# Second FFN of a hybrid decoder block: operand sums on GpSimd with two block sets, another order of the down passes, residual rows by quadrants, and PSUM copies of weights from the third pair on

## What is computed

```
gate, up = split(h @ w_up)            # w_up 1024 x 5632
y = (silu(gate) * up) @ w_down        # w_down 2816 x 1024
```

## Time and profile before

| | us |
|---|---|
| median of 3 runs (lowest, highest) | 2317.22 (2316.52, 2319.8) |
| the profiled execution | 2315.68 |
| its span in the profile | 2313.8 |
| TensorE busy (share of the span) | 2233.2 (97%) |
| VectorE busy | 1639.1 (71%) |
| ScalarE busy | 954.7 (41%) |
| GpSimd busy | 604.8 (26%) |
| mean granted TensorE clock | 0.987 |

### The profile page before, as it was taken

How to read it: one execution, slowest core, us unless ns; L and a number is a source line. 1 busy time by engine, 2 the same in 40 slices (tenths; PEclk the granted TensorE clock), 3 DMA queues, 4 the chain that set the end, 5 groups by cost and what they waited for, 6 DMA issues and landing times.

```text
span 2313.8 us, 32138 instructions
## 1 busy us (share of the span) xinstructions
PE 2233.2 (97%) x10370; PEld 1839.2 (79%) x10370; DVE 1639.1 (71%) x2145; ACT 954.7 (41%) x1555; POOL 604.8 (26%) x680
## 2 busy tenths in 40 slices
PE   7999999999999999999999899999999999999998
PEld 6788888888788887777787677887877888887886
DVE  5877777655555899999898737653496777765667
ACT  5555555445543122222223122334445555553444
POOL 2888999400000000000000150000333455541000
PEclk9999999999999999999999899999999999999999
DMA  6224444386763234444335432545445566658664
GB/s 167 73 82 133 143 141 139 121 274 194 256 198 123 89 121 151 127 126 136 105 112 180 153 125 78 164 152 185 164 141 180 201 204 204 204 204 299 195 193 173
DMA packets 298523, 370.61 MB, mean 160 GB/s; under 512 B 26457, under 2 KB 198577, under 8 KB 298064
## 3 DMA queue, kind: packets, MB, share of 16 engines
q1 hardware_dynamic: 279376, 300.24, 40.6%
q0 software_dynamic: 19056, 69.42, 8.4%
q10 hardware_dynamic: 16, 0.00, 0.0%
HBM read 259.73 MB, written 107.50 MB: 159 GB/s over the span
## 4 chain that ended last, share of the span: by engine, by line
PE 72%; DVE 19%; issue 4%; DMA 3%; ACT 2%; SPq 1%; POOL 0%; DVEq 0%; ACTq 0%; POOLq 0%
PE PU L1283 10%; PE PU L1285 10%; PE PU L1284 10%; DVE XT L2282 8%; PE PU L1224 5%; PE PU L1226 5%; PE PU L1225 5%; PE PU L1164 3%; PE PU L1163 3%; PE PU L1165 3%; PE PD L1163 3%; PE PD L1164 3%; PE PD L1165 3%; DVE TMP L2360 1%; PE PD L1358 1%
## 5 line engine op out<-in xcount | busy, mean ns | idle before, releaser
L1224 PE MATMUL PU<-Hhi,Whi 128*128 128x512 f32 x896 | 355.6, 397 | 9.8 <-DVE Hlo L2308 6.2
L1226 PE MATMUL PU<-Hhi,Wlo 128*128 128x512 f32 x896 | 351.7, 393 | 0.0
L1225 PE MATMUL PU<-Hlo,Whi 128*128 128x512 f32 x896 | 351.5, 392 | 0.0
L2282 DVE SCALAR_TENSOR_TENSOR XT<-XT,wq 128x1024 f32<-128x1024 f32 x240 | 309.3, 1289 | 7.8
L1043 POOL TENSOR_TENSOR RT<-XT 128x512 f32<-128x512 f32 x2 | 2.9, 1448 | 869.6 <-DMA XT<-d_conv 869.5
L1224 PEld LDWEIGHTS PU<-Hhi,Whi 128*128 128x128 f32 x896 | 170.1, 190 | 49.1 <-DVE Hlo L2308 7.8
L1225 PEld LDWEIGHTS PU<-Hlo,Whi 128*128 128x128 f32 x896 | 170.3, 190 | 35.4 <-issue 0.7
L1226 PEld LDWEIGHTS PU<-Hhi,Wlo 128*128 128x128 f32 x896 | 169.8, 189 | 36.0
L1283 PE MATMUL PU<-Hhi,Dhi 128*128 128x512 f32 x480 | 188.2, 392 | 5.6 <-ACT s1b L1630 5.6
L1285 PE MATMUL PU<-Hhi,Dlo 128*128 128x512 f32 x480 | 187.9, 391 | 0.0
L1284 PE MATMUL PU<-Hlo,Dhi 128*128 128x512 f32 x480 | 187.9, 391 | 0.0
(11 more groups left out here) (401 smaller groups left out, 5268.5 us busy)
## 6 DMA issues: line engine op xcount, KB each, us to landing
d_act<-G SPq DMA_DIRECT2D x88, 256.0 KB, 2.1
XT<-in_w_ffn_down SPq DMA_DIRECT2D x88, 256.0 KB, 3.3
XT<-d_act SPq DMA_DIRECT2D x88, 256.0 KB, 3.5
Wraw<-in_w_ffn_up SPq DMA_DIRECT2D x80, 256.0 KB, 4.5
XT<-in_w_ffn_up SPq DMA_DIRECT2D x80, 256.0 KB, 4.3
Wraw<-in_w_in SPq DMA_DIRECT2D x32, 512.0 KB, 6.0
Wraw<-d_sb SPq DMA_DIRECT2D x55, 256.0 KB, 2.7
TAB<-in_w_ffn_down POOLq DMA_DIRECT2D x11, 1024.0 KB, 5.3
```

Source lines behind the costliest of these rows:

```text
L1224: mm(o_, Whi[s][:, side, k, :], Hhi[:, k, hs[h]], start=k == 0, stop=False)
L1225: mm(o_, Whi[s][:, side, k, :], Hlo[:, k, hs[h]], start=False, stop=False)
L1226: last = mm(o_, Wlo[s][:, side, k, :], Hhi[:, k, hs[h]], start=False, stop=k == KT - 1)
L2282: stt(CVb, z_, w_, CVb, ALU.mult, ALU.add).then_inc(m["conv"], 1)
```

## The change

- PSUM copies: pairs 0 and 1 (those that are unrolled, with integer numbers) now both use SBUF for the low part; the copies to PSUM begin with the third pair. Both FFNs.
- `plain_act(r0, g0, 1, 1)` is issued one subtraction (`minus(2, 2, 1)`) earlier on VectorE. Both FFNs.
- The sums on GpSimd start when the weights of pair 1 are split, and use two block sets, XT[:, 6:8] and TAB in turn; the load for take k+2 is issued behind the sums of take k.
- D_ORD begins 3, 5, 7 instead of 7, 5, 3; pass 0 waits for weight sums step by step and for saved activations, pass 1 for activation sums.
- The residual rows come in four quadrants of 1 MB, behind steps (0,4), (0,7), (1,4) and (2,4); `gather` waits for them in passes 1, 2 and 4. One group of final squares moves from pass 3 to pass 2.

The core of the diff:

```diff
-D_ORD = (7, 5, 3, 4, 1, 2, 6)
+D_ORD = (3, 5, 7, 4, 1, 2, 6)
+D_ROWS = ((0, 1), (1, 1), (0, 0), (1, 0))
...
+            if p == 0:
+                sp.wait_ge(sb_st, 48 * (t + 1))
             sp.wait_ge(rd_lo, n - (RING - 1))
             sp.dma_start(raw_d(FFN2, slot), weights).then_inc(rd_raw[slot], 16)
             if p == 0:
+                sp.wait_ge(act_saved[0], 16 * (FT + 2 * t + 1))
+            if p == 1:
                 sp.wait_ge(sa_st, 48 * (t + 1))
             sp.wait_ge(ra_lo, n - (FFN2.z0 - FFN2.a0 + RING - 1))
...
-        sp.wait_ge(sb_st, 48 * FI)
...
+        ROWS_AT = ((0, 4), (0, 7), (1, 4), (2, 4))
+
+        def rows_after_mix(h, dh):
             sp.wait_ge(x_st, 16 * 2 * J)
             sp.wait_ge(u_prod, 7 * 2 * NSP)
-            load_rows(FFN2, h, d_x2)
+            sp.wait_ge(sa_st, 48 * (FI - 1))
+            sp.dma_start(XT[:, 4 * h:4 * h + 4, hs[dh]], d_x2[4 * h:4 * h + 4, :, hs[dh]].rearrange("j c d -> c j d"))\
+                .then_inc(xr_ld, 16)
...
-                if (p, t) in ((0, 6), (1, 6)):
-                    rows_after_mix(p)
+                if (p, t) in ROWS_AT:
+                    rows_after_mix(*D_ROWS[ROWS_AT.index((p, t))])
...
+        set_of = lambda k: (XT[:, 6:8, :].rearrange("p j n -> p (j n)"), TAB[:, 0:4 * HW])[k % 2]
+        TAKES = [("w", 0)] + [t for c in range(FI) for t in ((("w", c + 1),) if c + 1 < FI else ()) + (("a", c),)]
+        made = lambda k, kind: 48 * sum(1 for t in TAKES[:k] if t[0] == kind)
+
+        def stored(k):
+
+            wait(pool, sb_st, made(k, "w"))
+            wait(pool, sa_st, made(k, "a"))
+
+        def load_take(k):
+
+            kind, c = TAKES[k]
+            stored(max(k - 1, 0))
+            if kind == "w":
+                src = w_ffn2_down[0][2 * c * P:(2 * c + 2) * P].rearrange("(a p) n -> p a n", p=P)
+            else:
+                for h in range(2):
+                    pool.wait_ge(act_saved[h], 16 * (FT + 2 * c + 2))
+                src = rows_p(d_act[2 * c:2 * c + 2])
+            pool.dma_start(set_of(k).rearrange("p (a n) -> p a n", a=2), src).then_inc(pool_ld[k % 2], 16)
...
+        def take(k):
+
+            kind, c = TAKES[k]
+            blocks = set_of(k)
+            b0, b1, b2, b3 = [at4(blocks, i) for i in range(4)]
+            halves = lambda a: blocks[:, a * HW:(a + 2) * HW].rearrange("p (a n) -> p a n", a=2)
+            pool.wait_ge(pool_ld[k % 2], 16 * (k // 2 + 1 + (0 if k % 2 else KT)))
+            stored(k)
...
+            if k + 2 < len(TAKES):
+                load_take(k + 2)
 
         pool.wait_ge(rd_lo, FFN2.z0)
-        weight_sums(0)
-        for c in range(FI):
-            if c + 1 < FI:
-                weight_sums(c + 1)
-            act_sums(c)
+        pool.wait_ge(u_lo, 7 * (UBASE[FFN2] + 2))
+        pool.wait_ge(t_lo, 8)
+        for k in range(2):
+            load_take(k)
+        for k in range(len(TAKES)):
+            take(k)
...
-                    if (p, t) == (3, 7):
-                        fin_squares(0, 1, 2, 0)
+                    if (p, t) == (2, 7):
+                        fin_squares(0, 1, 1, 0)
...
-            if not (isinstance(p, int) and p == 0):
-                if isinstance(p, int) and p == 1 and POS[x] <= 3:
-                    act.wait_ge(c_in, 8)
-                    act.wait_ge(*norm_at("nf1" if S is FFN1 else "nf2", "lo", 2 * KT))
-                else:
-                    act.wait_ge(u_lo, q * 7 + HELD_BEFORE[POS[x]])
+            if not isinstance(p, int):
+                act.wait_ge(u_lo, q * 7 + HELD_BEFORE[POS[x]])
...
-                        if t == 2 and p in (1, 3):
-                            dve.wait_ge(xr_ld, {1: 80, 3: 96}[p])
+                        if t == 2 and p in (1, 2, 4):
+                            dve.wait_ge(xr_ld, {1: 96, 2: 112, 4: 128}[p])
...
-            if not (isinstance(p, int) and p == 0):
-                dve.wait_ge(u_hc, q * 7 + (POS[x] - (7 if S is FFN1 else 14)))
+            if not isinstance(p, int):
+                dve.wait_ge(u_hc, q * 7 + (POS[x] - (14 if S is FFN1 else 28)))
...
             minus(3, 2, 3)
+            plain_act(r0, g0, 1, 1)
             dve.wait_ge(t_add, t0 + 6)
             minus(2, 2, 1)
-            plain_act(r0, g0, 1, 1)
```

More of the change, by code:

```diff
@@ L338, in build @@
     ba_saved, ca_saved, rot_saved = sem("ba_saved"), sem("ca_saved"), sem("rot_saved")
-    small_saved, pool_ld = sem("small_saved"), sem("pool_ld")
+    small_saved, pool_ld = sem("small_saved"), sems("pool_ld", 2)
     norm = {k: sem("norm_" + k) for k in ("sq", "rs", "xn", "tr", "hi", "lo")}
@@ L736, in _ @@
             store_half(FFN2, NSP - 1, h)
-        def rows_after_mix(h):
+        ROWS_AT = ((0, 4), (0, 7), (1, 4), (2, 4))
+        def rows_after_mix(h, dh):
             sp.wait_ge(x_st, 16 * 2 * J)
             sp.wait_ge(u_prod, 7 * 2 * NSP)
-            load_rows(FFN2, h, d_x2)
+            sp.wait_ge(sa_st, 48 * (FI - 1))
+            sp.dma_start(XT[:, 4 * h:4 * h + 4, hs[dh]], d_x2[4 * h:4 * h + 4, :, hs[dh]].rearrange("j c d -> c j d"))\
+                .then_inc(xr_ld, 16)
         def store_out(h):
@@ L979, in tile_table @@
             r4 = slice(q * PR, (q + 1) * PR)
-            pool.dma_start(small4, d_small[:, :, r4, :]).then_inc(pool_ld, 16)
+            pool.dma_start(small4, d_small[:, :, r4, :]).then_inc(pool_ld[0], 16)
             pw_ = [[PW[:, a, 0:nt, r4].rearrange("p t r -> p r t").unsqueeze(3).to_broadcast([P, PR, nt, SG])
@@ L1014, in tile_table @@
             step(g.tensor_copy(M8q, M8[:, r4]))
-            pool.wait_ge(pool_ld, q * 16 + 16)
+            pool.wait_ge(pool_ld[0], q * 16 + 16)
             cs = TAB[:, T_COS:T_M8].rearrange("p (a r c) -> p a r c", a=2, c=C)
@@ L1052, in _ @@
         pool.dma_start(GF, norm_final_g.partition_broadcast(P)).then_inc(b_["fin_ld"], 16)
-        blocks = TAB[:, 0:4 * HW].rearrange("p (a n) -> p a n", a=2)
-        b0, b1, b2, b3, extra1, extra2 = [at4(TAB, i) for i in range(6)]
+        extra1, extra2 = at4(TAB, 4), at4(TAB, 5)
         extras = TAB[:, 4 * HW:6 * HW].rearrange("p (a n) -> p a n", a=2)
-        halves = lambda a: TAB[:, a * HW:(a + 2) * HW].rearrange("p (a n) -> p a n", a=2)
         rows_p = lambda ap: ap.rearrange("a p n -> p a n")
[L1060 to L1065, removed]
@@ L1067, in weight_sums @@
-        def weight_sums(c):
-            take(w_ffn2_down[0][2 * c * P:(2 * c + 2) * P].rearrange("(a p) n -> p a n", p=P), (c, max(c - 1, 0)), max(2 * c, c + 1))
-            step(g.tensor_tensor(extra1, b0, b3, ALU.add))
[L1071 to L1091, removed]
@@ new lines, in take @@
+        def take(k):
[5 more added lines that the diff above has]
+            stored(k)
+            step(g.tensor_tensor(extra1, b0, b3, ALU.add))
+            if kind == "w":
+                step(g.tensor_tensor(extra2, b2, b3, ALU.add))
+                pool.dma_start(rows_p(d_sb[c, B_T1:B_T7 + 1]), extras).then_inc(sb_st, 16)
+                step(g.tensor_tensor(b2, b2, b0, ALU.subtract))
+                step(g.tensor_tensor(b3, b1, b3, ALU.subtract))
+                pool.dma_start(rows_p(d_sb[c, B_T4:B_T3 + 1]), halves(2)).then_inc(sb_st, 16)
+                step(g.tensor_tensor(b1, b0, b1, ALU.add))
+                pool.dma_start(d_sb[c, B_T6], b1).then_inc(sb_st, 16)
+            else:
+                step(g.tensor_tensor(extra2, b0, b2, ALU.add))
+                pool.dma_start(rows_p(d_sa[c, A_S1:A_S5 + 1]), extras).then_inc(sa_st, 16)
+                step(g.tensor_tensor(b0, b1, b0, ALU.subtract))
+                step(g.tensor_tensor(b1, b1, b3, ALU.add))
+                pool.dma_start(rows_p(d_sa[c, A_S6:A_S2 + 1]), halves(0)).then_inc(sa_st, 16)
+                step(g.tensor_tensor(b2, b2, b3, ALU.subtract))
+                pool.dma_start(d_sa[c, A_S7], b2).then_inc(sa_st, 16)
+            if k + 2 < len(TAKES):
+                load_take(k + 2)
```

## The result

| | before | after |
|---|---|---|
| median, us (lowest, highest; 11 runs each) | 2317.22 (2315.3, 2320.54) | 2323.97 (2318.64, 2328.19) |
| ratio after / before, 95% interval | | 1.0024 [1.0015, 1.0033] |
| profiled execution, us | 2315.68 | 2324.92 |
| its span, us | 2313.8 | 2322.9 |
| mean granted TensorE clock | 0.987 | 0.985 |

The changed kernel is slower by 0.24% by the ratio (the medians differ by 6.75 us, 0.29%): inside the range (2309.0 to 2326.5), 5.4 us above the predicted 2318.6, and just over the 0.2% line.

A forecast was written before the change was run, and what follows sets the result against it. TensorE was busy 97% of the span, so only its idle or slow time could be won. Terms -1.3 - 5.7 + 8.4 = +1.4 us gave a median of 2318.6 us, 8 in 10 range 2309 to 2326.5.

The forecast's parts named there:

- (e): End of GpSimd's queue: last activation load stands ahead of block 9's sums, which start 2091.7 and land 2104.4 us.
- (f): Pass 0: SP's row wait holds step 5's operands; TensorE idles 13.2 us plus 2.2 slow matmuls, 8.4 us lost.
- (a): plain_act move, both FFNs: 1.32 us stop goes, VectorE's chain 0.6 us later, first FFN's pair 1 0.3 us later.
- (b): First FFN, pair 1 without PSUM copies: product 7 starts at 109.7, not 111.02, 1.3 us gained; 0.5 lost if clock falls.
- (c): Second FFN start without GpSimd's sums: product 7 of pair 1 starts at 1731.7, not 1737.44; 5.7 us gained.
- (d): Two block sets: a GpSimd take costs 14 us until caught up, some 20 before; TensorE indifferent, nothing taken.
- slower by VectorE: Rival: in the catch-up, 1731 to about 1890, denser sums make TensorE wait each pair; +8 us, 2326.6; chance 0.13.
- more than 2 us between 1760 and 2080: Sign that the forecast is wrong: TensorE idling more than this in the second FFN's up products.
- (g): Other moves, final squares a pass earlier and rows in four pieces: no effect, TensorE runs through from 2115.
- The faster one: Rival: smaller row loads remove the old stop in pass 0, nothing replaces it; 2303.2, milder case 2310.2; chance 0.17.
- The rival with a second stop: Rival: rows and late stores ahead of step 8 stop TensorE again, clock falls; +5 us, 2323.8; chance 0.12.
- the edits do nothing: Rival: the start is bound by pair 1's DMA, (b) and (c) fall; +8.4 us, 2325.6; chance 0.05.

The follow-up runs named there:

- Both experiments on it: The two runs last load behind (2314.37 us) and rows late (2315.74 us), each one edit to the changed kernel.
- before with copies from the third pair: Kernel before, only the copies to PSUM beginning at the third pair, GpSimd's sums in their old place: 2318.26 us, ratio 1.0007.
- plain_act back: Changed kernel with the plain block's multiplication put back behind the subtraction: 2322.74 us, ratio 1.0011.
- joined: Changed kernel with the last activation load behind block 9's sums, first two row loads behind (0,9) and (1,0), plain_act in its old place: 2306.46 us, 0.9947.
- joined gated: The joined kernel, GpSimd's sums of takes 11 to 19 also held until VectorE has made S16 of the coming pair: 2304.34 us, 0.9944.
- last load behind: Changed kernel, only GpSimd's load of activation block 10 moved behind the sums of block 9: 2314.37 us, ratio 0.9982.
- rows late: Changed kernel, only the first two row loads and their wait moved behind steps (0,9) and (1,0): 2315.74 us, ratio 0.9986.
- sums gated: The last load behind kernel, GpSimd's sums of takes 11 to 19 held until S16 of the coming pair is made: 2311.91 us, 0.9976.
- before with plain_act early: Kernel before, only plain_act(r0, g0, 1, 1) issued one subtraction earlier: 2324.45 us, ratio 1.0028.
- copies back: Changed kernel with the PSUM copies of pair 1 restored: 2325.07 us, ratio 1.0028.

## Why the prediction was near, and where it failed

The forecast (+1.4 us) was the sum -1.3 - 5.7 + 8.4. Against its own execution after had +9.1, the medians of all runs differ by 6.75, and the interval of the ratio allows 3.5 to 7.6.

- **(e), (f), the turn: right.** Block 9's sums from 2091.7 (measured 2091.88), landed 2104.4 (SP goes on at 2103.65), TensorE on at 2113 (2113.04), idle 13.2 (13.34), slow matmuls 2.2 (2.6). +8.4 against +9.3 in the ledger. Both experiments on it confirm the cause.
- **(a), (b) and (c) in one table.** Time from the first matmul of pair 0 to ScalarE's copy of pair 2's first product, less that of before, in us. A star marks a kernel whose granted clock fell behind the wait at product 7 of pair 1.

| kernels | first FFN | second FFN |
|---|---|---|
| pair 1 from SBUF, plain_act late: before with copies from the third pair | -1.4 | +4.3* |
| the same, sums late: plain_act back, joined, joined gated | -1.1, -1.3, -1.5 | -4.1*, -5.8, -5.6 |
| pair 1 from SBUF, plain_act early, sums late: after, last load behind, rows late, sums gated | +0.8*, +1.4*, -0.7, +1.2* | -3.3*, -5.3, -5.2, -3.6* |
| pair 1 through PSUM, plain_act early: before with plain_act early; copies back (sums late) | +1.4; +2.5 | +5.0*; -4.1 |

- **(c), the start of the second FFN: mechanism right, and the size nearly so where the clock held.** Product 7 of pair 1 was put at 1731.7 and began at 1732.36, 5.1 us earlier than before where 5.7 was written. Last load behind and rows late, the same code up to there, then lead by 5.3 and 5.2 us at pair 2. After leads by 3.3, since behind the 2.26 us wait the clock fell. The text had bounded this for (b) and forgot it for (c).
- **(b): mechanism right, the bound came true.** Where plain_act stays late, the first FFN is 1.1 to 1.5 us shorter in four kernels. The 1.3 of the text counts (a)'s delay in; with that delay and a held clock 0.7 is left (rows late). In after product 7 began at 110.59 instead of 109.7, of which 0.5 us stands before pair 0 begins (72.49, in before 72.01); then the clock fell behind the wait of 2.08, which is the bound that the text gives. The seven splits of pair 1 took 0.69 to 0.81 us in the first FFN of after, 0.3 us too much in all, so the 2.6 us that the weighing names did not come. In the second FFN the part alone loses 4.4 us, in the state that the kernel before leaves.
- **(a): undersized.** The delay of VectorE's chain is there as described (T3lo 0.5 us later from pair 0's start), but it costs 0.6 us in the first FFN where the clock held (rows late against the four with plain_act late), not 0.3. In the other three with plain_act early the clock fell too, which makes it 2 to 3 us. The medians of after and plain_act back differ by 1.2 us, a hint. On the kernel before the part costs 6.6 us, 4.6 of them in the second FFN by the ledger, because it releases GpSimd's first activation sums 2.3 us earlier; that was seen nowhere in the prediction. The stop it removes (1.32 us) was not on the path that sets the end.
- **(d): "TensorE is indifferent ... I take nothing" failed.** It cost 2.2 us from pair 13 on, and some 1 us in between. The rival that came nearest, slower by VectorE, had the right contention and the wrong criterion. It put the loss in the catch-up and made it depend on VectorE's share of time; it came after the catch-up, at a fixed phase, with 77% busy. The condition "more than 2 us between 1760 and 2080" was not met in idle time (1.4 us).
- **(g): nothing, right** as far as the spans show: no stop behind 2113.
- **The rivals.** The faster one needed the order in (e) not to matter. It does in the change as written, and it doesn't in joined, which comes out at 2306.5, between that rival's 2303.2 and 2310.2. The rival with a second stop names 2323.8 (by its own terms 2323.6), almost the measured median, but that is chance: the second stop did not occur in after; "the edits do nothing" falls with the 5.1 us.

So the sum came near because its largest term, the loss at the turn, was right. Its two gains (-1.3 and -5.7) measured +0.7 and -0.5 in the ledger: three things ate them, (a), the clock behind product 7 of pair 1, and the sums from pair 13 on, and none of the three was in the sum at its size.

**What stays open.** Whether the clock falls behind the product-7 wait. Eight profiled kernels have this wait in the first FFN at 2.06 to 2.11 us (clock fell in three) and seven in the second at 2.25 to 2.28 (fell in three); a fall costs 1.5 to 2.1 us by the next pair. After and rows late run the same code up to there, and one fell and the other didn't. All three falls of the first FFN are among the four kernels with plain_act early, none among the four with it late; in the second FFN it is two of four and one of three. With so few executions that is a hint, and no run tells what decides it.

## What to carry to other kernels

Before a wait goes into an in-order queue, list what is queued behind it and when the thing waited for can be made at the latest; where that thing stands behind another wait in a second queue, the order of two lines there can be worth 10 us. A VectorE chain with both inputs in SBUF took nearly three times as long beside GpSimd (5.9 us, alone 2.1), so what matters is at which phase of the loop the two meet, not how busy either is: start GpSimd's work behind the operation TensorE waits for. When an operation moves, follow everything that it releases, on every engine: plain_act freed a PSUM half for TensorE, and a load for GpSimd. And a part of a change should be priced in the state that the other parts leave, since here the PSUM copies' part costs 4.4 us of the second FFN without the sums' part.

## What was not expected of the hardware

- The same code with a wait of 2.06 us and of 2.08 us kept and lost the clock, while the prediction had put a border between 2.00 and 2.59.
- A subtraction of 128x2048 took 2.29 us alone and 3.27 to 3.61 beside GpSimd's additions, and GpSimd's additions stretched too, from 1.3 to as much as 3.2 us: either of the two can be the one that is held up.
- Code that no kernel here touches differs between profiled executions by more than most of the edits are worth: the stretch with the mixer by up to 7.9 us.
